# The second feed-forward network as seven block products for eight, its hidden blocks sent through memory to a second phase

## What is computed

```python
def second_block(x, ...):
    ...
        h = rmsnorm(x, norm2_g[l])
        x = x + (jax.nn.silu(h @ w_gate[l]) * (h @ w_up[l])) @ w_down[l]
    return x
```

## Time and profile before

| | |
|---|---|
| time, median of 3 runs | 2449.34 us (2445.32 to 2454.12) |
| profiled execution: span | 2447.8 us; the page gives no time around it |
| PE busy | 2379.5 us of it, 97% |
| DVE, ACT, POOL busy | 1258.1, 823.3, 354.9 us |
| norm and first four tiles of the network | about 1698 to 1760.3 us |
| the rest of the network on PE | 1760.3 to 2438.5 us |
| last transposes, copies, stores | 2438.5 to 2447.8 us |

### The profile page before, as it was taken

How to read it: one execution, slowest core, us unless ns; L and a number is a source line. 1 busy time by engine, 2 the same in 40 slices (tenths; PEclk the granted TensorE clock), 3 DMA queues, 4 the chain that set the end, 5 groups by cost and what they waited for, 6 DMA issues and landing times. The chain is left out here.

```text
span 2447.8 us, 28497 instructions
## 1 busy us (share of the span) xinstructions
PE 2379.5 (97%) x10880; PEld 1921.4 (78%) x10880; DVE 1258.1 (51%) x1500; ACT 823.3 (34%) x1232; POOL 354.9 (14%) x276
## 2 busy tenths in 40 slices
PE   7999989999999999999999999989999999999999
PEld 5788887777888888888877767768888888888887
DVE  6468267447455444444465489964433333323334
ACT  5232358544222222221244478852311111111111
POOL 1120045222000000000033356631000000000000
PEclk9999999999999999999999999999999999999999
DMA  8256422222111111111133220021111111111111
GB/s 329 71 183 227 144 87 61 104 69 78 52 52 43 51 51 42 44 51 49 46 122 124 69 78 18 17 88 47 48 52 52 43 51 51 43 43 51 51 51 69
DMA packets 192734, 183.79 MB, mean 75 GB/s; under 512 B 8505, under 2 KB 170633, under 8 KB 192145
## 3 DMA queue, kind: packets, MB, share of 16 engines
q1 hardware_dynamic: 189984, 175.21, 22.4%
q0 software_dynamic: 2208, 7.37, 0.9%
q10 hardware_dynamic: 465, 0.17, 0.0%
HBM read 154.38 MB, written 28.34 MB: 75 GB/s over the span
## 5 line engine op out<-in xcount | busy, mean ns | idle before, releaser
L295 PE MATMUL ps<-hhi,whi 128*128 128x512 f32 x1696 | 664.1, 392 | 6.8 <-DVE arena L3282 3.5
L296 PE MATMUL ps<-hlo,whi 128*128 128x512 f32 x1696 | 661.3, 390 | 0.0
L297 PE MATMUL ps<-hhi,wlo 128*128 128x512 f32 x1696 | 661.0, 390 | 0.0
L219 DVE TENSOR_TENSOR wlo<-raw,whi 128x1024 fp32r<-128x1024 f32 x178 | 226.3, 1273 | 386.4 <-ACT whi L214 386.3
L295 PEld LDWEIGHTS ps<-hhi,whi 128*128 128x128 f32 x1696 | 319.0, 188 | 75.3 <-DVE arena L3282 3.9
L296 PEld LDWEIGHTS ps<-hlo,whi 128*128 128x128 f32 x1696 | 319.1, 188 | 67.4 <-issue 1.2
L297 PEld LDWEIGHTS ps<-hhi,wlo 128*128 128x128 f32 x1696 | 319.2, 188 | 66.7
L214 ACT ACTIVATE whi<-raw 128x1024 fp32r<-128x1024 f32 x178 | 184.6, 1049 | 386.3 <-PE ps L2565 286.5
L2717 DVE TENSOR_TENSOR arena<-arena,ps 128x1024 f32<-128x1024 f32 x152 | 185.4, 1220 | 129.0 <-PE ps L2565 128.1
L2563 PE MATMUL ps<-hid_hi,whi 128*128 128x512 f32 x608 | 237.6, 391 | 0.0
L2564 PE MATMUL ps<-hid_lo,whi 128*128 128x512 f32 x608 | 236.7, 389 | 0.0
(11 more groups left out here) (365 smaller groups left out, 3361.4 us busy)
## 6 DMA issues: line engine op xcount, KB each, us to landing
raw<-in_w_up SPq DMA_DIRECT2D x66, 512.0 KB, 3.8
raw<-in_w_down SPq DMA_DIRECT2D x44, 512.0 KB, 3.6
raw<-in_w_in SPq DMA_DIRECT2D x32, 512.0 KB, 5.0
arena<-in_w_ada SPq DMA_DIRECT2D x32, 512.0 KB, 5.5
raw<-in_w_gate SPq DMA_DIRECT2D x22, 512.0 KB, 3.7
raw<-in_w_out SPq DMA_DIRECT2D x16, 512.0 KB, 3.9
arena<-x_park SPq DMA_DIRECT2D x2, 4096.0 KB, 12.2
x_park<-arena SPq DMA_DIRECT2D x4, 2048.0 KB, 8.9
```

Source lines behind the costliest of these rows:

```text
L219: nc.vector.tensor_tensor(wlo[:, w.off % RING, :], raw[:, w.off % RAW, :], whi[:, w.off % RING, :].bitcast(F32), ALU.subtract).then_inc(lo ...
L295: nc.tensor.matmul(acc[:, tok], whi[:, s, ws], hhi[:, k, tok], start=(k == 0), stop=False)
L296: nc.tensor.matmul(acc[:, tok], whi[:, s, ws], hlo[:, k, tok], start=False, stop=False)
L297: mm = nc.tensor.matmul(acc[:, tok], wlo[:, s, ws], hhi[:, k, tok], start=False, stop=(k == DK - 1))
```

## The change

The up and the down product are each computed by one level of Strassen's algorithm (Winograd's form). A pair of tiles is a 2 by 2 block matrix (gate, up; first and second 512 input channels), and the input is one too (channels; token halves). Seven products of blocks, with sums of blocks as operands, take the place of eight. Pairs 0 and 1 stay as they are; pairs 2 to 21 go the new way.

Sums that this needs: of weights, four per pair on POOL (`pool_weights`); of the input, sixteen once (`pool_operands`), for which the norm's output is kept in `kept`; of hidden rows, four per two pairs (`pool_hidden`); of w_down, four per step for 22 steps (`pool_down`, in pairs 3 and 5 two steps). Sums of products are made by DVE and ACT. The seven hidden blocks of two pairs are stored to memory (256 KB each), and the four sums of w_down as well. x is stored before, since the sums of the input lie over it, and loaded back.

The second phase has 77 units, 7 products by 11 pairs of hidden tiles. A unit loads one weight block and one hidden block (256 KB each), splits both on ACT and DVE, and has 12 matmuls on PE. Nothing loops: every instruction is written out.

The core of the diff, with the functions that the prediction speaks of:

```diff
-N_TILES = T_FF2 + N_FF
+N_TILES = T_FF2 + 4
+        class SecondNorm(HalfNorm):
+            def park(self, sp):
+                for h in range(2):
...
+                    sp.dma_start(x_park[:, :, half(h)], xt[:, :, half(h)]).then_inc(self.parked, 16)
+        class SplitFeedForward:
+            SUM_AT = {1: 2, 2: 3, 4: 1, 6: 4}
+            T_OF = {1: 2, 2: 3, 4: 1, 5: 4}
+            T_SPLITS = [(i, k) for k in range(4) for i in (1, 3, 2)] + [(4, k) for k in range(4)]
+            DOWN = (("S", 0, 4), ("A", 0, 0), ("A", 1, 1), ("S", 3, 3), ("S", 1, 5), ("S", 2, 2), ("A", 2, 6))
+            UNITS = 7 * Q
+            def steps_of(self, j):
+                extra = {3: 1, 5: 1}
+                at = sum(1 + extra.get(i, 0) for i in range(2, j))
+                return range(at, at + 1 + extra.get(j, 0))
+            def store_hidden(self, sp, q):
+                    self.summed(sp, 2 * q - 1, "product1")
...   (three stores)
+                sp.wait_ge(F["hsum"], 4 * q + 4)
...   (four stores)
+            def load_down_rows(self, sp, s):
+                if s:
+                    sp.wait_ge(self.F["dstored"], 32 * s)
...
+            def load_unit(self, sp, u):
+                F, (i, q) = self.F, divmod(u, self.Q)
+                if u >= 4:
+                    sp.wait_ge(F["lo"], 2 * (u - 4) + 2)
...
+            def sp(self, sp):
+                self.lead.sp(sp)
+                self.load_pair(sp, 2)
+                self.norm.park(sp)
+                sp.wait_ge(lo_done, self.base + 4 + RAW)
+                self.load_pair(sp, 3)
+                for j in range(2, self.PAIRS):
+                    if j + 2 < self.PAIRS:
+                        sp.wait_ge(F["wlo"], 7 * (j - 2) + 6)
+                        sp.wait_ge(F["wsum"], 4 * (j - 2) + 4)
+                        self.load_pair(sp, j + 2)
+                    steps = self.steps_of(j)
+                    self.load_down_rows(sp, steps[0])
+                    if j % 2 == 0:
+                        self.store_hidden(sp, j // 2 - 1)
+                    self.store_down_sums(sp, steps[0])
+                    for s in steps[1:]:
+                        self.load_down_rows(sp, s)
+                        self.store_down_sums(sp, s)
+                sp.wait_ge(F["wlo"], 7 * (self.PAIRS - 2))
+                sp.wait_ge(F["dstored"], 32 * 2 * self.Q)
+                sp.wait_ge(F["stored"], 112 * (self.Q - 1))
+                for u in range(self.UNITS):
+                    if u == 7:
+                        self.store_hidden(sp, self.Q - 1)
+                    if u == self.Q - 1:
+                        sp.wait_ge(F["stored"], 112 * self.Q)
+                    self.load_unit(sp, u)
+                    if u == self.Q - 1:
+                        sp.dma_start(self.x_in, x_park).then_inc(F["x_in"], 16)
+            def pe_pair(self, pe, j):
+                for e in range(7):
+                    z = (0, 1, 2, 0, 1, 2, 3)[e]
+                    pe.wait_ge(F["wlo"], 7 * n + e + 1)
...
+                    elif e == 5:
+                        self.copied(pe, n, "c7")
...
+                    for k in range(4):
+                        if n == 0 and e in self.T_OF:
+                            pe.wait_ge(F["tlo"], self.T_SPLITS.index((self.T_OF[e], k)) + 1)
...   (three matmuls)
+            def act(self, act):
+                act.wait_ge(self.norm.parked, 32)
...
+                for j in range(2, self.PAIRS):
+                    def ahead(e):
+                        if j < last:
+                            self.act_weight(act, j + 1, e)
+                        elif e:
+                            for u in ((0, 1) if e == 1 else (e,)):
+                                self.act_unit(act, u)
...   (copy of product 0)
+                    ahead(0)
+                    ahead(1)
+                    act.wait_ge(F["mm"], 7 * n + 3)
+                    nc.scalar.activation(self.val_of(j)[:, half(1)], self.bank(j, 2), ACT.Copy).then_inc(F["copied"], 1)
+                    ahead(2)
...
+            def dve_weight(self, dve, j, e):
+                dve.wait_ge(F["whi"], 7 * n + e + 1)
+                nc.vector.tensor_tensor(self.wl(e), self.weight(j, e), self.wh(e).bitcast(F32), ALU.subtract).then_inc(F["wlo"], 1)
+            def dve(self, dve):
...
+                    if j > 2:
+                        self.dve_last_block(dve, j - 1)
+                    ahead(0)
+                    dve.wait_ge(F["mm"], 7 * n + 2)
+                    self.copied(dve, n, "c1")
+                    nc.vector.tensor_tensor(v[:, half(0)], g[:, half(1)], self.bank(j, 1), ALU.add).then_inc(F["summed"], 1)
+                    ahead(1)
+                    if j > 2:
+                        self.dve_product(dve, j - 1, 1)
+                    ahead(2)
+                    ahead(3)
+                    dve.wait_ge(F["mm"], 7 * n + 5)
+                    nc.vector.tensor_tensor(g[:, half(1)], g[:, half(1)], self.bank(j, 1), ALU.add).then_inc(F["summed"], 1)
+                    self.summed(dve, n, "u4")
+                    self.copied(dve, n, "c7")
+                    nc.vector.tensor_tensor(v[:, half(1)], v[:, half(1)], g[:, half(1)], ALU.add).then_inc(F["summed"], 1)
+                    ahead(4)
...
+                    nc.vector.tensor_tensor(v[:, half(0)], v[:, half(0)], self.bank(j, 2), ALU.add).then_inc(F["summed"], 1)
+                    self.dve_product(dve, j, 0)
+                    ahead(5)
+                    ahead(6)
+            def pool_weights(self, pool, j):
+                pool.wait_ge(F["raw" + str(j % 2)], 32 * (n // 2 + 1))
+                if n:
+                    pool.wait_ge(F["wlo"], 7 * n)
+                self.pool_link(pool, "wsum", 4 * n + 1, nc.gpsimd.tensor_tensor(s1, a21, a22, ALU.add))
+                self.pool_link(pool, "wsum", 4 * n + 2, nc.gpsimd.tensor_tensor(s2, s1, a11, ALU.subtract))
+                nc.gpsimd.tensor_tensor(s3, a21, a11, ALU.subtract).then_inc(F["wsum"], 1)
+                nc.gpsimd.tensor_tensor(s4, a12, s2, ALU.subtract).then_inc(F["wsum"], 1)
+            def pool_operands(self, pool, k):
+                pool.wait_ge(self.norm.op_lo, DK + k + 5)
...   (four of 128x512)
+            def pool(self, pool):
+                self.lead.pool(pool)
+                self.pool_weights(pool, 2)
+                for k in range(4):
+                    self.pool_operands(pool, k)
+                for j in range(2, self.PAIRS):
+                    if j + 1 < self.PAIRS:
+                        self.pool_weights(pool, j + 1)
+                    if j % 2 == 0:
+                        self.pool_hidden(pool, j // 2 - 1)
+                    for s in self.steps_of(j):
+                        self.pool_down(pool, s)
+                self.pool_hidden(pool, self.Q - 1)
...   (twelve additions of x)
-        ffn2 = feed_forward("ffn2", T_FF2, xt, False, out2, norm2_2, finish=Output())
+        ffn2 = SplitFeedForward("ffn2", T_FF2, xt, out2, norm2_2, a["w_gate_2"], a["w_up_2"], 0, a["w_down_2"], Output())
```

More of the change, by code:

```diff
@@ L126, in sem, with retire @@
             return sems[name]
+        def retire(prefix):
+            gone = [sems.pop(n) for n in list(sems) if n.startswith(prefix)]
+            cleared.extend(gone)
+            return gone
         def clear(pool, names):
@@ L143, in block_kernel @@
         causal = sb("causal", [P, P])
-        selF = sb("selF", [ML_H, ML_H, P])
         small = sb("small", [P, 64])
         identR = sb("identR", [P, P], F32R)
-        bandR = sb("bandR", [P, 2, 2 * P], F32R)
-        gateR = sb("gateR", [P, 2, DK, 64], F32R)
+        with nc.sbuf_tensor("selF", [P, ML_H, P], F32) as select_rows, nc.sbuf_tensor("bandR", [P, 2, 2 * P], F32R) as bandR, \
+             nc.sbuf_tensor("gateR", [P, 2, DK, 64], F32R) as gateR, nc.sbuf_tensor("gateF", [P, DK, 64], F32) as gateF:
+            pass
+        selF = select_rows[0:ML_H, :, :]
+        shared = sb("shared", [P, 2560])
         raw = sb("raw", [P, RAW, D])
@@ L170, in block_kernel @@
              nc.sbuf_tensor("hid_lo", [P, 4, T], F32R) as hidlo:
+            pass
+        with nc.sbuf_tensor("sum_hi", [P, DK, T], F32R) as sum_hi, nc.sbuf_tensor("sum_lo", [P, DK, T], F32R) as sum_lo:
             pass
@@ L709, in __init__, with operand @@
                 self.scaled, self.op_hi, self.op_lo = (sem(name + x) for x in ("_scaled", "_hi", "_lo"))
+                self.parked = sem(name + "_x_parked")
                 if self.rounds == 2:
-                    self.y_scaled, self.x_sum, self.parked = (sem(name + x) for x in ("_y_scaled", "_added", "_x_parked"))
+                    self.y_scaled, self.x_sum = (sem(name + x) for x in ("_y_scaled", "_added"))
+            def operand(self, k, tok):
+                return cbuf[:, k % 2, tok] if self.keep is None else self.keep[:, k, tok]
             def sums(self, r, h):
@@ L813, in dve_operands @@
                     if k < DK:
-                        if k >= 2:
```

(9 more changed lines are left out.)

407 lines of the change are left out of this document (399 added, 8 removed).

## The result

| | before | after |
|---|---|---|
| median of 4 runs | 2448.7 us (2445.32 to 2454.12) | 2384.57 us (2383.49 to 2388.45) |
| ratio, 95% interval | 1 | 0.9734 (0.9717 to 0.9751) |
| span of the profiled execution | 2447.8 us | 2381.7 us |
| first new product starts on PE | (first four tiles done at 1760.3) | 1757.0 us |
| from there to the end | 687.5 us | 624.7 us |

The forecast was 2400 (range 2372 to 2440). The changed kernel ran once more later, in five runs beside other runs of before: 2386.78 us, ratio 0.973 (0.9717 to 0.9743).

The account below looks back on a forecast made before the run. It took PE's number of matmuls to bound the network. From the median 2449.3 us, -84.3 + 5 + 15 + 11 + 3.5 = -49.8 gave 2399.5, so 2400; range 2372 to 2440.

Parts of the forecast that it names:

- the 84.3 us: PE over the new products: 372 fewer matmuls at 0.2267 us each save 84.3 us, the most the change can give.
- the floor: Time from first new product to the end without the 84.3 us of matmuls and without added waits: 603.2 us.
- Start of the new phase (5 us): Before the first new product: PE waits 3.5 us for POOL's sums and the splits, with half clock 5 us.
- Pairs 2 to 7 (15 us): Sixth product of early pairs: PE waits for ACT's copy of product 2 behind POOL's late sums, 15 us in all.
- The recursion: Pairs 2 to 7: POOL's begin computed pair by pair, delays summing to 19.4 us at 1.7 per operation, taken as 15.
- The 1.7: POOL's effective us per operation, from 1.4 alone plus 0.3 to 0.4 lost, with some 9 of 10 meeting a DVE operation.
- Change of phase (11 us): Pair 21: PE waits for product 2's copy, behind first units' splits and w_down's last sums, 9.5 us plus 1.6 clock.
- Units 7 and 11 (3.5 us): Second phase: unit 7 about 1 us late for the last hidden rows, unit 11 about 2.5 behind x's 4 MB load.
- The quick POOL (2381): Rival: POOL's operations take 1.4 us and stay hidden beside PE, giving 2381 us; chance 0.22.
- Exclusion throughout (2427): Rival: POOL and DVE shut each other out for whole records, a pair takes 20.4 us for 19.04, giving 2427; chance 0.16.
- A wait in every pair (2480): Rival: POOL about 3.5 us late in each pair, with half clock 5 us a pair, giving 2480, slower; chance 0.08.

Follow-up runs that it names:

- the sums done early: Changed kernel with w_down's extra steps in pairs 9, 13, 17, none in 21, x loaded in eight pieces, last hidden stores ahead of unit 10's load: 2372.44 us, ratio 0.9663.
- all three edits: Changed kernel with w_down's extra steps in pairs 13 and 15, units 0 to 3 split behind product 2's copy, x loaded in eight pieces: 2381.97 us, ratio 0.9718.
- the units behind the copy: Changed kernel with ACT and DVE splitting units 0 to 3 behind product 2's copy in the last pair, not before it: 2389.92 us, ratio 0.9747.

## Why the prediction was right, and what it mis-sized

**What bounds the kernel, and the 84.3 us: right.** Matmuls are still 0.227 us apart, 372 are gone, the run without POOL's sums comes within 1.5 us of the floor, and putting 240 matmuls back costs them again less the waits that they cover.

**Start of the new phase (5 us): smaller, 1.0 to 1.5.** The prediction put 20 operations in a row from 1729.5 on, four sums of weights and sixteen of the input. But the four came earlier, for pair 2's loads were issued at 1707.54 and not behind 1721.92:

```profile
1714.42 1.27 POOL L3874 TENSOR_TENSOR arena<-shared 128x512 f32<-128x512 f32 x1 [1.42 <-DMA shared<-in_w_up]
```

The sixteen ran from 1727.28 to 1753.8, where the prediction's row ends at 1763.5. Of these 9.7 us the four operations are 6.8, the earlier begin 2.2, and the rest the average, about 1.65 and not 1.7. The wait was so short that no halved clock followed.

**Pairs 2 to 7 (15 us): this is the term that failed, measured 5.0.** The recursion took each operation of `pool_down` as 128x512 at 1.7 us. They are 128x256, as `load_down_rows` brings them in, and take 0.74 us where nothing meets them and 0.82 to 1.04 on average. A step costs 3.6 us for 6.8. With that alone, at 1.7 for the others, an even pair is 6.8 + 6.8 + 3.6 = 17.2 us and pairs 3 and 5 are 6.8 + 3.6 + 6 + 3.6 = 20.0; POOL begins pair 3 at 9.3 + 17.2 - 19.0 = 7.5 and pair 4 at 8.5, before the 8.9 from which PE would wait at the sixth product, and no pair is late there. In the trace POOL begins at 8.7, 8.3, 8.1, 8.3 and 7.9 us in pairs 2 to 6. The 1.7 was too much as well: 1.5 on average. And the halved clock behind such waits was left out of the 15. What the mechanism would do with long steps, w_down's sums done twice shows: 5.6 and 5.7 there. The waits that came instead, at the fourth product of pairs 3, 5 and 7, the prediction had not: it followed POOL's sums of weights to ACT, and not its hidden sums, whose stores free a buffer for DVE, which stands before ACT's copy. Moving the extra steps showed that those of pairs 5 and 7 are of POOL's making; for that of pair 3 no experiment was made but the one without sums, where it is gone. It stays in the kernel with the sums done early, which has no double step before pair 9.

**Change of phase (11 us): 5.9 and 2.5 of clock, 8.4.** Place, releaser and chain as predicted. It was shorter by the narrow last steps: from the begin of pair 20 the last sum of w_down ended at 28.6 us, the prediction had 34.7. The prediction took 1.6 for the clock, from one idle time; here it was 2.5, in the second profile of the same kernel 2.0 after a longer wait, 6.7.

**Units 7 and 11 (3.5 us): 4.4 and 1.7 of clock, 6.1.** Nothing at unit 7 in the kernel after, but only since pair 21 held PE back; with that wait removed unit 7 had 7.3. Unit 11 was late for x as predicted; x took 15.7 us to land, where the row of before had 12.2.

**The sum.** -84.3 + 1.0 + 5.0 + 8.4 + 6.1 = -63.8, where the medians differ by 2448.7 - 2384.57 = 64.1 us. That they agree so closely is chance, since the spans vary by more. The forecast's four terms were too high by 4.0, 10.0 and 2.6 us and, the last, too low by 2.6, which made up for part of the others.

**The rivals.** The quick POOL (2381) was nearest in time, and right in part: POOL isn't undisturbed, but at 1.49 us per 128x512 operation it was nearer to that rival's 1.4 than to the prediction's 1.7, which holds only for those that meet a DVE operation; and it has less to do than both reckoned. Exclusion throughout (2427): the exclusion is there, POOL's record beside DVE is 1.62 for 1.29 and DVE's remainder 1.18 for 0.69 on average; but it doesn't cover the whole record, and POOL's chain sets no pair between 1877 and 2130 us. The Trainium skill (SBUF — State Buffer, section on who interferes with whom) says that, of a VectorE instruction with two SBUF inputs and a GpSimd one that reads SBUF, one fully blocks the other. The runs agree in that the two take turns, one operation each, and in that DVE isn't slowed with a PSUM input, but a turn was 1.64 us, not the 1.98 of two whole records. A wait in every pair (2480): no trace of it.

## What to carry to other kernels

Where an engine off the critical path is to take on much work, count its operations by their width as the code slices them, and follow each of its products to all that wait in order behind it, stores and freed buffers too, not only the nearest operand. A wait that is removed where the bottleneck meets a late chain comes back at the next place where it meets it: splitting the first units later lost 2.5 us and, with the other two edits, gained nothing over one of them alone, and doing the chain's work earlier, in stretches where its engine had room, gave the time back. Before a big transfer is put in a queue of small ones with due times, cut it in pieces of their size: here that took away a wait of 4.4 us with its clock, 6.7 us of the stretch in one profile each.

## What was not expected of the hardware

- Two operations that exclude each other, POOL's of 128x512 with two SBUF inputs and DVE's, take turns of 1.64 us side by side, where their steps alone are 1.22 and 0.61, sum 1.83, and their records 1.29 and 0.69. So the exclusion costs less than either sum, and a semaphore between POOL's operations changes nothing of it.
- How long the half clock lasts doesn't follow from the idle time before it. Matmuls stood more than 0.3 us apart for 5.6 us after 5.87 us of waiting in the kernel after, for 4.0 after 6.74 in its second profile, for 3.6 after 7.37 with all three edits, for 6.1 after 3.04 with the units behind the copy. Over all waits of 3 us and more it was 3.1 to 6.1 us. After waits up to 1.8 us the matmuls were 0.23 us apart from the second on; after 2.93 us, with w_down's sums twice, they were so once and once not.
- The time ahead of the edited part varied by 8 us between the profiles, though nothing there was edited, more than most experiments moved. Starting the count at the first new product brought two profiles of one kernel to within 0.5 us.
